# Seven half products in all six feed-forward stages of a two-block transformer kernel, with bank waits moved and a low part on GpSimd

## What is computed

```
def swiglu(x, w13, w2):
    a, b = jnp.split(x @ w13, 2, axis=-1)
    return (jax.nn.silu(a) * b) @ w2
...
        x = layer_norm(ALPHA * x + swiglu(x, ffn_w13[layer], ffn_w2[layer]), ...)
...
def swiglu_2(x, w_gate, w_up, w_down):
    return (jax.nn.silu(x @ w_gate) * (x @ w_up)) @ w_down
...
        h = h + 0.5 * swiglu_2(rmsnorm(h, ffn1_norm[i]), ffn1_w_gate[i], ffn1_w_up[i], ffn1_w_down[i])
...
        h = h + 0.5 * swiglu_2(rmsnorm(h, ffn2_norm[i]), ffn2_w_gate[i], ffn2_w_up[i], ffn2_w_down[i])
```

## Time and profile before

| | |
|---|---|
| median of 3 runs | 3596.53 us (3596.45 to 3596.96) |
| profiled execution | 3596.28 us, span 3594.5 us |
| TensorE matmul, weight load | 3470.0 us (97%), 2823.0 us (79%) |
| VectorE, ScalarE, GpSimd | 1861.5 us (52%), 1427.0 us (40%), 418.7 us (12%) |
| memory traffic | 288.22 MB read, 2.10 MB written |

### The profile page before, as it was taken

How to read it: one execution, slowest core, us unless ns; L and a number is a source line. 1 busy time by engine, 2 the same in 40 slices (tenths; PEclk the granted TensorE clock), 3 DMA queues, 4 the chain that set the end, 5 groups by cost and what they waited for, 6 DMA issues and landing times. The chain is left out here.

```text
span 3594.5 us, 45464 instructions
## 1 busy us (share of the span) xinstructions
PE 3470.0 (97%) x17188; PEld 2823.0 (79%) x17212; DVE 1861.5 (52%) x2779; ACT 1427.0 (40%) x2212; POOL 418.7 (12%) x338
## 2 busy tenths in 40 slices
PE   9999899999999999999999999999999998999998
PEld 7787788877778986888886688886888886678886
DVE  3386767666676766333266733325333257733335
ACT  4343534444553535332344533225332244533324
POOL 0001000010200001221001022102221001022102
PEclk9999999999999999999999999999999999999999
DMA  4201222322022322333220132313233220123322
GB/s 146 87 1 36 76 94 90 96 88 81 24 77 94 101 87 72 99 94 112 84 84 19 53 99 94 117 64 94 94 99 104 84 85 23 53 94 99 111 70 76
DMA packets 80376, 292.63 MB, mean 81 GB/s; under 512 B 8912, under 2 KB 11728, under 8 KB 79952
## 3 DMA queue, kind: packets, MB, share of 16 engines
q1 hardware_dynamic: 79632, 289.31, 25.1%
q10 hardware_dynamic: 576, 1.05, 0.1%
HBM read 288.22 MB, written 2.10 MB: 81 GB/s over the span
## 5 line engine op out<-in xcount | busy, mean ns | idle before, releaser
L158 DVE TENSOR_TENSOR w_low<-w_raw,w_high 128x1024 fp32r<-128x1024 f32 (+3 forms) x395 | 500.9, 1268 | 1220.8 <-ACT w_high L153 1220.7
L192 PE MATMUL bank<-x_high,w_high 128*128 128x512 f32 x2216 | 870.4, 393 | 20.0 <-DVE w_low L158 7.2
L194 PE MATMUL bank<-x_high,w_low 128*128 128x512 f32 x2216 | 863.1, 389 | 0.0
L193 PE MATMUL bank<-x_low,w_high 128*128 128x512 f32 x2216 | 862.9, 389 | 0.0
L153 ACT CAST w_high<-w_raw 128x1024 fp32r<-128x1024 f32 (+3 forms) x395 | 421.6, 1067 | 759.9 <-PE bank L194 750.2
L192 PEld LDWEIGHTS bank<-x_high,w_high 128*128 128x128 f32 x2216 | 416.4, 188 | 120.3 <-DVE w_low L158 11.1
L193 PEld LDWEIGHTS bank<-x_low,w_high 128*128 128x128 f32 x2216 | 416.6, 188 | 86.8 <-issue 1.7
L194 PEld LDWEIGHTS bank<-x_high,w_low 128*128 128x128 f32 x2216 | 416.2, 188 | 87.0
L192 PE MATMUL bank<-hidden_high,w_high 128*128 128x512 f32 x1056 | 411.7, 390 | 6.4 <-DVE w_low L1175 6.4
L193 PE MATMUL bank<-hidden_low,w_high 128*128 128x512 f32 x1056 | 411.0, 389 | 0.0
L194 PE MATMUL bank<-hidden_high,w_low 128*128 128x512 f32 x1056 | 410.8, 389 | 0.0
(11 more groups left out here) (609 smaller groups left out, 5185.4 us busy)
## 6 DMA issues: line engine op xcount, KB each, us to landing
w_raw<-in_stream SPq DMA_DIRECT2D x413, 512.0 KB, 3.5
w_raw<-in_stream SPq DMA_DIRECT2D x64, 704.0 KB, 4.0
w_raw<-in_stream SPq DMA_DIRECT2D x32, 384.0 KB, 3.1
w_raw<-in_stream SPq DMA_DIRECT2D x4, 576.0 KB, 3.8
dft_positions<-in_dft SPq DMA_DIRECT2D x2, 1024.0 KB, 4.8
w_raw<-in_stream SPq DMA_DIRECT2D x16, 128.0 KB, 2.1
out<-result SPq DMA_DIRECT2D x4, 512.0 KB, 2.7
h<-in_x ACTq DMA_DIRECT2D x4, 256.0 KB, 6.4
```

What stands on the lines that cost most here:

```text
L158: self.nc.vector.tensor_tensor(self.lo[:, j % 2, 0:size], self.raw[:, j % RAW_SLOTS, 0:size], self.hi[:, j % 2, 0:size].bitcast(F32), ALU. ...
L192: nc.tensor.matmul(out, lhs[0], rhs[0], start=start, stop=False)
L193: nc.tensor.matmul(out, lhs[0], rhs[1], start=False, stop=False)
L194: return nc.tensor.matmul(out, lhs[1], rhs[0], start=False, stop=stop)
```

## The change

`Seven` takes over all that the feed-forward stages have in common, both kinds of stage call it, and the four second-block stages now go by seven half products too, in the same three stretches. Weights of all six are packed in the same order of jobs (`seven_jobs`). In detail:

- TensorE: the wait for join 12 of pair n-2 moves from before A11(n) to before S1(n); join 11 of pair n-2 gets a wait of its own before A12(n). The first four tiles go to banks 0 to 3. The last two tiles of down jobs 0 and 1 go in the order tile 7 of job 0, tile 7 of job 1, tile 6 of job 0, tile 6 of job 1.
- GpSimd: `hidden_low` of every hidden tile, in the first-block stages too (there it was VectorE's).
- ScalarE: in the first pair of a stretch copy 2 comes before part A12; in the opening, copy 1 of pair 0 comes before the high halves of the last input sum and of the first hidden tiles.
- VectorE: join 12 comes before the S4 sum. In the second-block stages `scale` multiplies each gate quarter by `rstd` between join and SiLU, and the down result is first scaled by `rstd` into a buffer and then added to `h`.
- Second-block opening: ScalarE scales the first four input tiles by the gain, in halves, after the `rstd` chain; VectorE makes the input sums from these. Input splitting and the first two jobs are interleaved tile by tile.

```diff
-                        if n >= 2:
-                            if n % 2:
-                                pe.wait_ge(S.quarter_hid, V.quarter("21", n - 2))
-                            else:
-                                pe.wait_ge(S.quarter_gated, V.quarter("21", n - 2))
-                            pe.wait_ge(S.joined, V.joined("12", n - 2))
...
+            if n >= 2:
+                if n % 2:
+                    pe.wait_ge(S.quarter_hid, self.quarter("21", n - 2))
+                else:
+                    pe.wait_ge(S.quarter_scaled if self.rstd is not None else S.quarter_gated,
+                               self.quarter("21", n - 2))
...
+            self.pe_product(pe, S, n, "A11", "Y", True, False)
+            if n >= 2:
+                pe.wait_ge(S.joined, self.joined("11", n - 2))
+            self.pe_product(pe, S, n, "A12", "X", True, True)
+            if n > a:
+                self.pe_a22(pe, S, n - 1)
+            pe.wait_ge(S.copied, self.copied(1, n))
+            self.pe_product(pe, S, n, "S2", "Y", False, False)
+            if n > a:
+                self.pe_s4(pe, S, n - 1)
+            if n >= 2:
+                pe.wait_ge(S.joined, self.joined("12", n - 2))
...
+            self.pe_product(pe, S, n, "S1", "Z", True, False)
+            pe.wait_ge(S.copied, self.copied(2, n))
+            self.pe_product(pe, S, n, "S3", "Y", False, False)
...
+    def act_pairs(self, act, S, f, opening=None):
...
+            self.act_copy(act, S, 1, n)
+            if n == 0 and opening:
+                opening()
+            if n < b:
+                self.act_part(act, S, "A11", n + 1)
+            else:
+                self.act_high(act, S, c, self.down_at[f])
+            if n == a:
+                self.act_copy(act, S, 2, n)
+            if n > a and up:
+                self.act_silu(act, S, "22", n - 1)
+            if n < b:
+                self.act_part(act, S, "A12", n + 1)
+            if not up:
+                self.act_silu(act, S, "11", n)
+            self.act_part(act, S, "A22", n)
+            if n > a:
+                if up:
+                    self.act_silu(act, S, "21", n - 1)
+                else:
+                    self.act_hidden(act, S, f, n - 1, 1)
+                self.act_copy(act, S, 2, n)
+            if n < b:
+                self.act_part(act, S, "S2", n + 1)
...
+    def dve_scale(self, dve, S, q, n):
+        if self.rstd is None:
+            return
...
+        self.nc.vector.tensor_tensor(self.gated[:, t, c], src, self.rstd[:, c],
+                                     ALU.mult).then_inc(S.quarter_scaled, 1)
...
+    def pool_hidden(self, pool, S):
...
+                    self.nc.gpsimd.tensor_tensor(self.hlo[:, x, :], self.hidden[:, t, :],
+                                                 self.hhi[:, x, :].bitcast(F32), ALU.subtract).then_inc(S.hid_low, 1)
...
+    def dve_pairs(self, dve, S, f, opening=None):
...
+            if n < b:
+                self.dve_sum(dve, S, "S1", n + 1)
+                self.dve_sum(dve, S, "S2", n + 1)
+            if n > a:
+                self.dve_join(dve, S, "22", n - 1)
+            if n < b:
+                self.dve_part(dve, S, "A11", n + 1)
+            if n > a and up:
+                self.dve_scale(dve, S, "22", n - 1)
+            if n < b:
+                self.dve_part(dve, S, "A12", n + 1)
+            if n > a and not up:
+                self.dve_multiply(dve, S, "22", n - 1)
+            self.dve_join(dve, S, "11", n)
+            if n == b:
+                self.dve_low(dve, S, c, self.down_at[f])
+            if not up:
+                self.dve_scale(dve, S, "11", n)
+            self.dve_part(dve, S, "A22", n)
+            if n > a:
+                if up:
+                    self.dve_scale(dve, S, "21", n - 1)
+                else:
+                    self.dve_multiply(dve, S, "21", n - 1)
+            if up:
+                self.dve_multiply(dve, S, "11", n)
+            if n < b:
+                self.dve_sum(dve, S, "S3", n + 1)
+                self.dve_part(dve, S, "S2", n + 1)
+            else:
+                self.dve_low(dve, S, c + 1, self.down_at[f] + 1)
+            self.dve_part(dve, S, "S4", n)
+            if n > a:
+                self.dve_join(dve, S, "12", n - 1)
+            if n < b:
+                self.dve_sum(dve, S, "S4", n + 1)
+            if n > a and up:
+                self.dve_scale(dve, S, "12", n - 1)
+            if n < b:
+                self.dve_part(dve, S, "S1", n + 1)
+            if n > a and not up:
+                self.dve_multiply(dve, S, "12", n - 1)
+            if n < b:
+                self.dve_part(dve, S, "S3", n + 1)
...
+        pe.wait_ge(S.hid_low, 1 + 2 * end)
+        self.pe_down_tile(pe, S, f, 0, tiles - 1, False, False)
+        self.pe_down_tile(pe, S, f, 1, tiles - 1, False, False)
+        pe.wait_ge(S.hid_low, 2 + 2 * end)
+        self.pe_down_tile(pe, S, f, 0, tiles - 2, False, True)
+        self.pe_down_tile(pe, S, f, 1, tiles - 2, False, True)
...
+                rstd_chain(nc, C, act, S, C.bank[summed or 6])
+                for q in range(4):
+                    for x, at in ((t_a, early), (t_c, late)):
+                        nc.scalar.activation(x[:, q, :], C.h[:, q, at], ACT.Identity,
+                                             scale=gain(q)).then_inc(S.x_scaled, 1)
...
+                V.act_high(act, S, 2, 2)
+                act.wait_ge(S.t_sums, 1)
+                V.act_t(S, thi[:, 0, :, :], t_b)
+                V.act_high(act, S, 3, 3)
...
+                dve.wait_ge(S.x_scaled, 8)
+                nc.vector.tensor_tensor(t_b, t_c, t_a, ALU.subtract).then_inc(S.t_sums, 1)
+                dve.wait_ge(S.t_sums, 1)
+                for q in range(4):
+                    nc.vector.scalar_tensor_tensor(t_c[:, q, :], C.h[:, 4 + q, late], gain(4 + q), t_c[:, q, :],
+                                                   ALU.mult, ALU.subtract).then_inc(S.t_sums, 1)
+                V.dve_low(dve, S, 2, 2)
...
+                    nc.vector.tensor_tensor(scaled, halves(C.bank[4 + d % 2][:, :]), halves(C.rstd[:, :]),
+                                            ALU.mult).then_inc(S.out_scaled, 1)
+                    dve.wait_ge(S.out_scaled, DT * f + d + 1)
+                    h = halves(C.h[:, d, :])
+                    nc.vector.scalar_tensor_tensor(h, scaled, scale, h, ALU.mult, ALU.add).then_inc(S.residual_done, 1)
```

More of the change, by code:

```diff
@@ new lines, in sync_pairs, with sync_down @@
+    def sync_pairs(self, sp, S, f):
+        for n in range(self.first[f], self.last[f] + 1):
+            sp.wait_ge(S.part_sums, self.summed("S4", n))
+            sp.wait_ge(S.part_low, self.made("A12", n))
+            self.refill(sp, self.job(n, 0))
+            sp.wait_ge(S.part_low, self.made("A22", n))
+            self.refill(sp, self.job(n, 1))
+    def sync_down(self, sp, S, f, first=0, last=DT):
+        for d in range(first, last):
+            sp.wait_ge(S.low_ready, self.ahead + self.classic + DT * f + d + 1)
+            self.refill(sp, self.down_at[f] + d)
@@ L844, in ffn_stage @@
-    ahead = jobs - plain
-    with ExitStack() as ctx:
[L846 to L855, removed]
+    with ExitStack() as ctx:
+        V = Seven(nc, ctx, C, 1, {"S2": 3, "A22": 5})
+        H, ahead, jobs, last_phase = V.HALF, V.ahead, V.jobs, len(PHASES) - 1
+        hidden, gated = V.hidden, V.gated
@@ L881, in pieces @@
[L881 to L889, removed]
+        thi, tlo = V.thi, V.tlo
+        with stage(nc, Seven.SEMS + Input.SEMS + Statistics.SEMS) as S, nc.Block() as block:
@@ L902, in _ @@
-                for f in range(len(PHASES)):
-                    for n in range(V.first[f], V.last[f] + 1):
-                        sp.wait_ge(S.part_sums, V.summed("S4", n))
-                        sp.wait_ge(S.part_low, V.made("A12", n))
-                        refill(V.job(n, 0))
-                        sp.wait_ge(S.part_low, V.made("A22", n))
-                        refill(V.job(n, 1))
-                    for d in range(DT):
-                        sp.wait_ge(S.low_ready, ahead + classic + DT * f + d + 1)
-                        refill(down_at[f] + d)
+                V.sync_classical(sp, S)
@@ L1427, in _ @@
             def _(act):
[L1428 to L1429 removed]
+                act.sem_inc(S.high_ready, ahead + 1)
+                if split:
                     for t in range(DT):
@@ L1520, in second_in_stage @@
+                for f in range(len(PHASES)):
+                    V.dve_pairs(dve, S, f, opening)
+                    for d in range(DT):
+                        residual(f, d)
+                        V.dve_down(dve, S, f, d)
+                        if f == last_phase:
+                            after.dve_adds(nc, C, dve, S, 0, d, None)
+    W.base += V.jobs
 def second_in_stage(nc, C, L, prj, mv, mix, lat_hi, lat_lo, M, qs, kn, v, heads):
```

974 lines of the change are left out of this document (465 added, 509 removed).

## The result

The changed kernel takes 3757.78 us (median of 4 runs, 3755.56 to 3759.64) against 3596.74 before: a ratio of 1.0442, 95% interval 1.0429 to 1.0455. Forecast were 3738 in 3665 to 3785, slower with a chance of 0.90. The profiled execution took 3755.56, its span is 3753.8, 159.3 more than before.

A forecast was written before the change was run, and what follows sets the result against it. VectorE's in-order list and its exchange with ScalarE, not TensorE, were taken as the bound. The sum 3596.3 + 150 (four second-block stages) - 6 (two first-block stages) gave 3740, stated as 3738, range 3665 to 3785 us.

The forecast's parts named there:

- VectorE's list with its trips: Stretch middles: VectorE's in-order operations plus idle for ScalarE's part_high (1.40 to 1.90 us per round trip) set the period.
- The rival by which TensorE binds: All six stages: A11's bank wait alone makes the stalls, so the kernel gets faster, 3520 us; chance 0.07.
- its bank wait: TensorE's wait for join 12 at A11: moving it gains -22 us per first-block stage if TensorE binds.
- four scales: Second-block pairs: rstd products between join (or bank) and SiLU on VectorE add 3.2 us per two pairs.
- GpSimd beside low halves: Per two pairs: GpSimd's hidden_low delays VectorE's next low halves by 1.29 us, bounds nothing to 1.57.
- The rival in which GpSimd never meets the list: All six stages: GpSimd's hidden_low costs VectorE nothing, 61 us less, 3677 us; chance 0.12.
- The three stretches: Half-product runs of a second-block stage: 213.8 us plus 23.7 for the longer groups, 237.5.
- the opening: Second-block stage start: four tiles 21.8 us, plus a wait of 4 where it splits x, 1 otherwise.
- The wait named: Second-block start where x is split: TensorE waits 4 us for the third job's halves, behind ScalarE scalings and VectorE sums.
- Forecast -3 a stage: First-block stages: -4.7 us in the first stretch from copy 1 going earlier, +1.8 at stretch ends.
- the 0.68 more idle that was costed: First-block stretch ends: down tile 0 ends one matmul triple before tile 1, not two; +0.6 us, three times.
- The clock rival: Second-block stretches: stalls drop TensorE to 1.2 GHz in a quarter of middle pairs, some +100, 3840 us; chance 0.06.

The follow-up runs named there:

- (9): Changed kernel without the second of three matmuls of every half product (the one with x's low half): 3693.0 us.
- (4): Changed kernel with ScalarE's order alone altered: each SiLU and hidden_high behind the next part's high half: 3569.9 us, 0.9924 of the kernel before.
- (5): Changed kernel with TensorE's wait for join 12 of two pairs before back at A11: 3756.0 us.
- experiment 2: Changed kernel without the four quarter products with rstd ahead of SiLU in second-block pairs: 3668.6 us.
- experiment 1: Changed kernel with the four second-block stages by whole tiles as in the kernel before: 3598.4 us, ratio 1.000.
- (12): Changed kernel with parts first on ScalarE, down tile 0 finished before tile 1's last triples, and hidden_low of the pairs back on VectorE: 3544.8 us, ratio 0.9856.

## Why the prediction was right, and where it was off

**The period.** That VectorE's list with its trips, not TensorE, makes the period is shown from both sides: a third of TensorE's matmuls gone leaves the group as it was (9), and the trips gone bring it to TensorE's 20.16 (4). The rival by which TensorE binds falls with its bank wait (5). The Trainium skill's rule to optimise the engine of highest occupancy first (Perfetto Trace Analysis, Identifying the Most-Contended Engine) names TensorE here: it led with 92% (weight loads 78%), against 67% for VectorE and 44% for ScalarE. The gain of 4 came from ScalarE's order, the least busy of the three.

**The group's terms.**

| term, us per two pairs | forecast | measured | from |
|---|---|---|---|
| first block | 22.6 | 22.42 | window |
| second block | 25.8 | 25.45 | window |
| four scales | 3.2 | 3.08 | experiment 2 |
| GpSimd beside low halves | 1.29 | 0.40 + 0.65 = 1.05 | 1.09 and 1.34 against 0.69 |

GpSimd's operations met the low halves as the list had it, with 0.54 and 0.79 left; each lost that less 0.14, the same 0.14 as in the earlier trace rows. By the Trainium skill (SBUF — State Buffer, Who interferes with whom) the later of the two waits for all of the earlier; these rows agree but for that 0.14. The rival in which GpSimd never meets the list falls.

**The second block.** The three stretches were forecast at 237.5 together; 72.49 + 95.25 + 69.67 = 237.4. The stages came out at 400.46 and 399.16 for 399 and 396. The term that was too small is the opening: the first half product starts 1450.42 - 1422.03 = 28.4 us into the stage that splits x, for 21.8 + 4. The wait named is there, shorter in the row than the whole loss, and behind it the granted clock was 0.50 for 3.42 us:

```profile
1437.82 0.50 PE L191 MATMUL bank<-x_high,w_high 128*128 128x512 f32 x1 [3.33 <-DVE w_low L1096]
...
1438.70:1442.12 3.42, 3.42 (x10) 2.65 (x9) 3.42 (x4) 2.47 (x5) 0.00 (x0) 0.50 0.70 195
```

**The first block.** Forecast -3 a stage, measured +0.32 and -0.36 (and 3598.4 in experiment 1). The 4.27 us idle in the opening is gone, and the first stretch is 3.28 shorter (69.92 to 66.64), not 4.7: a wait for part_low of the second pair takes part of its place. The end of a stretch got the 0.68 more idle that was costed (1.09 to 1.77), and the first stretch of the first stage more than that. The window of that stretch, and its two waits:

```profile
410.05:476.69 66.64, 59.48 (x482) 58.09 (x481) 55.64 (x93) 35.41 (x77) 9.61 (x6) 1.00 0.32 104
...
419.17 0.36 PE L905 MATMUL bank<-x_high,part_high 128*128 128x256 f32 x1 [1.77 <-DVE part_low L1102]
...
492.27 0.50 PE L191 MATMUL bank<-hidden_high,w_high 128*128 128x512 f32 x1 [1.77 <-DVE w_low L1096]
...
493.37 0.63 PE L192 MATMUL bank<-hidden_low,w_high 128*128 128x512 f32 x1
493.79 0.63 PE L193 MATMUL bank<-hidden_high,w_low 128*128 128x512 f32 x1
...
493.21:496.62 3.41, 3.41 (x10) 2.66 (x9) 0.74 (x1) 0.00 (x0) 0.00 (x0) 0.50 0.80 205
1059.82:1063.23 3.41, 3.41 (x18) 3.35 (x17) 2.95 (x5) 3.41 (x8) 0.00 (x0) 0.50 0.32 96
```

A microsecond after the 1.77 us of idle the granted clock falls to 0.50, the lower level, for 3.41 us; seven matmuls last 0.63 and start every 0.43 us instead of 0.227, a loss of some 1.5 us. In the second stage the same stands near the start of the first stretch (the last row). The kernel before had its time at the lower level in the opening (417.44 on); it did not go with the 4.27 us of idle but moved to another place, which the forecast had nowhere. Whether copy 2 ahead of part A12 costs a stretch's start its share was not tried apart.

**The sum.** The profiled execution is 15.6 above the forecast's 3740: 6 are the first block, some 6 the second block's stages (39.4, 39.9, 37.8 and 38.9 longer), the rest lies in front of and behind stages, where the hand-over grew by 0.5 to 0.8 at five places. The clock rival did not come as it was put: 1.00 in the middle of these stretches with TensorE 83% busy (21.17 of 25.45). But in the second-block stages the granted clock was 0.50 for 3.4 us five times, shortly after waits of 1.88 to 3.33 us, where the kernel before had it at 1.00. By the starts of matmuls that is some 1.5 us each time, an estimate of 8 us in all; no term of the sum has it, and without it the four stages would be some 148 us longer, for 150 forecast. One bound was added up wrongly: openings of 0 to 7 us instead of 4 and 1 give +18, not +14, which changes nothing here.

## What to carry to other kernels

When two engines pass work back and forth in order, look for the engine whose idle time ends on the other while that one had itself waited for the first; such round trips set the period though no engine is full, and an operation put inside one costs its wait as well as its time. The cure is often an order: put what the waiting engine asks for next ahead of what nobody needs yet. Here that was worth 188 us, and only after it and with hidden_low back on VectorE (12) were fewer matmuls worth anything in the second block, some 3 us a stage.

## What was not expected of the hardware

With a third of its matmuls left out TensorE was busy for 17.59 of 25.44 us and its granted clock fell to 0.88 in the middle of stretches, where 21.17 of 25.45 had kept 1.00. In the timeline of that kernel (experiment 9) matmuls start every 0.21 us, and after a short idle at full pace again:

```profile
1576.73 0.41 PE L905 MATMUL bank<-x_high,part_high 128*128 128x256 f32 x1
1576.95 0.41 PE L906 MATMUL bank<-x_high,part_low 128*128 128x256 f32 x1
1578.38 0.38 PE L905 MATMUL bank<-x_high,part_high 128*128 128x256 f32 x1 [1.02 <-ACT sq_sum_and_last L1009]
1578.60 0.28 PE L906 MATMUL bank<-x_high,part_low 128*128 128x256 f32 x1
1578.72 0.28 PE L905 MATMUL bank<-x_high,part_high 128*128 128x256 f32 x1
```

The two levels (1.2 and 2.4 GHz) take turns, and the group's time stays at 25.44: here the slower clock cost the group nothing, since TensorE wasn't its period.
